# Start bytes of the activation buffers within 64 bytes, in a two-block transformer kernel on one core

## What is computed

```python
for l in range(2):                                   # first block
    z = rms_norm(x, g) @ w_in[l]                     # 1024 -> 8200 columns
    y_rg, y_ml, y_xa = rg_lru(...), mlstm(...), memory_attention(...)
    x = x + (g0*(y_rg @ w_br_rg) + g1*(y_ml @ w_br_ml) + g2*(y_xa @ w_br_xa)) @ w_out
    x = x + (swiglu(h2, w1, w3, w2) if l == 0 else moe_swiglu(h2, router, 8 experts, top 2))
for l in range(2):                                   # second block, x and a context of 256 tokens
    x = x + mod * attention(...)                     # layer 0: also for the context
    x = x + mod * swiglu_2(h_x, ffn_w1, ffn_w3, ffn_w2)
return rmsnorm(x, final_g)
```

## Time and profile before

| | us |
|---|---|
| median of 3 runs (3346.85, 3349.06, 3357.35) | 3349.06 |
| profiled execution, whole | 3353.13 |
| its span | 3351.3 |
| TensorE busy (matmuls) | 3197.1 |
| VectorE busy | 2331.1 |
| ScalarE busy | 1828.2 |
| mean granted clock of TensorE | 0.977 |

### The profile page before, as it was taken

One profiled execution on the slowest core, in us unless ns is written; L12 is line 12 of the kernel. 1 busy time (PEld: TensorE's weight loads), 2 busy tenths in 40 slices (PEclk: granted clock), 3 DMA queues, 4 the chain that ended last, 5 costly groups with the idle time before them and its releaser, 6 DMA issues.

```text
span 3351.3 us, 56010 instructions
## 1 busy us (share of the span) xinstructions
PE 3197.1 (95%) x24147; PEld 2976.5 (89%) x24147; DVE 2331.1 (70%) x2984; ACT 1828.2 (55%) x2180; POOL 0.2 (0%) x4
## 2 busy tenths in 40 slices
PE   8999999999999899999999999989899999998898
PEld 7998999999889799999999999878777889985798
DVE  6877655577876588888888888755575556466555
ACT  5564544455545477777777777643464445335443
POOL 0000000000000000000000000000000000000000
PEclk9999999999999899999999999999899999998899
DMA  6433565454335699899899999632223466530353
GB/s 256 167 131 134 178 237 201 152 194 172 115 133 181 239 380 357 334 359 357 336 356 358 338 354 356 249 132 75 102 95 129 157 236 239 214 144 33 151 187 116
DMA packets 102812, 723.62 MB, mean 216 GB/s; under 512 B 11424, under 2 KB 13344, under 8 KB 16672
## 3 DMA queue, kind: packets, MB, share of 16 engines
q1 hardware_dynamic: 102560, 719.97, 58.0%
HBM read 718.87 MB, written 1.05 MB: 215 GB/s over the span
## 4 chain that ended last, share of the span: by engine, by line
PE 78%; DVE 11%; ACT 7%; issue 2%; DMA 1%; SPq 0%; DVEq 0%; ACTq 0%
PE PS L1639 14%; PE PS L1640 14%; PE PS L1641 14%; PE PS L1590 6%; PE PS L1592 6%; PE PS L1591 6%; DVE WL L2424 4%; ACT WH L2015 3%; PE PS L1951 3%; PE PS L1952 3%; PE PS L1953 3%; PE PS L1793 1%; PE PS L1694 1%; PE PS L1721 1%; PE PS L1937 1%
## 5 line engine op out<-in xcount | busy, mean ns | idle before, releaser
L2424 DVE TENSOR_TENSOR WL<-RAW,WH 128x2048 fp32r<-128x2048 f32 (+2 forms) x428 | 962.6, 2252 | 542.1 <-ACT WH L2015 538.7
L2015 ACT ACTIVATE WH<-RAW 128x2048 fp32r<-128x2048 f32 (+2 forms) x428 | 803.5, 1880 | 243.1 <-PE PS L1641 183.0
L1639 PE MATMUL PS<-PH,WH 128*128 128x256 f32 x2464 | 703.7, 286 | 22.5 <-ACT F L2097 6.1
L1640 PE MATMUL PS<-PL,WH 128*128 128x256 f32 x2464 | 694.9, 282 | 0.0
L1641 PE MATMUL PS<-PH,WL 128*128 128x256 f32 x2464 | 694.9, 282 | 0.0
L2424 DVE TENSOR_TENSOR WL<-F,WH 128x2048 fp32r<-128x2048 f32 x210 | 480.6, 2289 | 79.9 <-ACT WH L2015 79.2
L1639 PE MATMUL PS<-HPH,WH 128*128 128x256 f32 (+1 forms) x1648 | 493.9, 300 | 17.6 <-ACT WH L2015 8.7
L1639 PEld LDWEIGHTS PS<-PH,WH 128*128 128x128 f32 x2464 | 467.1, 190 | 29.2 <-issue 20.5
L1640 PE MATMUL PS<-HPL,WH 128*128 128x256 f32 (+1 forms) x1648 | 481.6, 292 | 0.0
L1641 PE MATMUL PS<-HPH,WL 128*128 128x256 f32 (+1 forms) x1648 | 481.3, 292 | 0.0
L1640 PEld LDWEIGHTS PS<-PL,WH 128*128 128x128 f32 x2464 | 467.3, 190 | 0.6
(11 more groups left out here) (397 smaller groups left out, 4925.3 us busy)
## 6 DMA issues: line engine op xcount, KB each, us to landing
F<-in_moe_w SPq DMA_DIRECT2D x210, 1024.0 KB, 5.3
RAW<-in_ffn_w SPq DMA_DIRECT2D x130, 1024.0 KB, 5.0
RAW<-in_moe_w SPq DMA_DIRECT2D x126, 1024.0 KB, 5.1
RAW<-in_w_in SPq DMA_DIRECT2D x64, 1024.0 KB, 4.9
F<-in_ada_w SPq DMA_DIRECT2D x18, 1024.0 KB, 11.3
RAW<-in_w_kv SPq DMA_DIRECT2D x16, 1024.0 KB, 4.9
G<-in_ada_w SPq DMA_DIRECT2D x15, 1024.0 KB, 9.1
RAW<-in_w_in_ab SPq DMA_DIRECT2D x12, 1024.0 KB, 5.7
```

The lines of the kernel that those rows point to most:

```text
L1639: T_.matmul(out, lh, rh, start=first, stop=False)
L1640: T_.matmul(out, lh, rl, start=False, stop=False)
L2015: S.activation(mem["WH"][:, t.s % NHL, 0:m], v.raws[t.slot][:, 0:m], ACT.Copy).then_inc(*ac.done("w_hi", t.s))
L2424: V.tensor_tensor(mem["WL"][:, t.s % NHL, 0:m], v.raws[t.slot][:, 0:m], mem["WH"][:, t.s % NHL, 0:m].bitcast(F32), sub).then_inc(*dv.done( ...
```

## The change

P[0] to P[2] become slices of one buffer PAIRS, cut so that both halves of a pair begin 12, 20 and 26 floats further than a multiple of 4096 floats; HP and HD become one buffer each with both halves cut 6 and 2 floats past its start. By the memory map PAIRS starts where PH0 did (180064, 32 past a multiple of 64), so P[0] begins 16, P[1] 48 and P[2] 8 bytes past a multiple of 64. HP starts at 117088 as before and its halves begin 24 bytes later, 56 past. HD starts at 165536 and its halves 8 bytes later, 40 past. HP is 64 bytes longer, so what stands behind it (BIAS to G3) moves by 64 bytes; EDGE keeps G4 and G5 clear of the longer HD and moves them by 128. RAW, WH, WL and YS stay. No instruction is added, taken away or reordered; only addresses differ.

```diff
-            mem["P"] = [(sb(f"PH{i}", [128, 8, T], F32R, s1), sb(f"PL{i}", [128, 8, T], F32R, s1)) for i in range(3)]
+            pairs = sb("PAIRS", [128, 6 * 8 * T + 26], F32R, s1)
+            at = [4096 * i + first for i, first in enumerate((12, 20, 26))]
+            mem["P"] = [tuple(pairs[:, a + 2048 * j:a + 2048 * j + 2048].rearrange("p (k t) -> p k t", k=8) for j in range(2)) for a in at]
...
-        mem["HP"] = (sb("HPH", [128, 8, 512], F32R), sb("HPL", [128, 8, 512], F32R))
+        hp = sb("HP", [128, 2 * 8 * 512 + 16], F32R)
+        mem["HP"] = tuple(hp[:, 6 + 4096 * j:6 + 4096 * j + 4096].rearrange("p (k t) -> p k t", k=8) for j in range(2))
...
-            mem["G"] = [sb(f"G{i}", [128, 4, 512], F32, s3)[:, :, :] for i in range(6)]
+            mem["G"] = [sb(f"G{i}", [128, 4, 512], F32, s3)[:, :, :] for i in range(4)]
+            sb("EDGE", [128, 16], F32, s3)
+            mem["G"] += [sb(f"G{i}", [128, 4, 512], F32, s3)[:, :, :] for i in (4, 5)]
...
-            mem["HD"] = (sb("HDH", [128, 8, 512], F32R, s4), sb("HDL", [128, 8, 512], F32R, s4))
+            hd = sb("HD", [128, 2 * 8 * 512 + 16], F32R, s4)
+            mem["HD"] = tuple(hd[:, 2 + 4096 * j:2 + 4096 * j + 4096].rearrange("p (k t) -> p k t", k=8) for j in range(2))
```

## The result

The changed kernel takes **3363.67 us** (median of five runs, 3361.18 to 3365.83) beside 3349.06 us of the kernel before (five runs, 3346.85 to 3357.35). The ratio is 1.0039, with a 95% interval of 1.0027 to 1.005: slower, by 14.6 us in the medians. The forecast was 3338 us and faster; the time lies in its range and on the side of the rival "slower" (3371 us, chance 0.30). The profiled execution took 3361.18 us, its span is 3359.4 us, 8.1 more than that of before.

The account below looks back on a forecast made before the run. TensorE was taken to bound the kernel, its time near a sum of matmul start-to-start distances. Matmuls moving shifted pairs gave 10.9 us less and all other terms 0, so 3349 - 11 = 3338 us, range 3275 to 3380.

Parts of the forecast that it names:

- the rival "slower": Stream and load share interleaved banks; new distances settle the matmuls moving shifted pairs at 120 ns: 3371 us, chance 0.30.
- What bounds the kernel, and that distances from start to start are its price: TensorE, busy 3197 of 3351 us, bounds the kernel; a matmul costs its start-to-start distance, 118.33 ns for most.
- The form "rows": 118.33 to 117.5 ns, 10.9 us less: The 13104 matmuls of 256 columns that move a shifted pair gain 0.83 ns each, 10.9 us less.
- the gate tile: Matmuls with 36-column loads and stationary starts 0, 16, 32, 48 past 64; their 117.5 ns priced the new layout.
- The bounds: Router runs with 8-column loads, 114 and 120 ns: matmuls moving shifted pairs gain 57 us or lose 22.
- The form "tok": 0: The 5328 matmuls that load a shifted pair, at 116.7 to 117.7 ns, change by 0; bounds 19 less, 13 more.
- 512 columns: 0: The 1632 matmuls with 512 columns, at 233.3 ns, change by 0; bounds 9 us less, 11 us more.
- L1922, L1962, L1963: 0: Some 100 to 250 matmuls of YS with PL2 leave equal starts, 119.4 ns; under 1 us, taken as 0.
- Copies: nothing: ScalarE and VectorE copies writing the pairs at 8 mod 16 cost nothing, as convolution steps take 481 and 480 ns.
- Its second estimate: Streams from 8 mod 16 touch 65 lines, not 64; 5712 matmuls moving HP and HD cost 10 us more.
- The rival "no change": Levels come from operand order, not place, and the excess from streaming: 3349 us, chance 0.22, plus 0.02 for other residues.
- The rival "much faster": Present places keep streams slow; new ones reach the router's 114 ns, 85 us less: 3265 us, chance 0.12.

Follow-up runs that it names:

- the maps: Kernels of back-to-back matmuls alone, computation left out, against no kernel, with start bytes of moving and stationary operands varied; 256-column levels from 113.3 ns up.
- e1_map: The first kernel of matmuls alone, in stretches of 96 with operand start bytes set by hand; the windows shown have 113.3 to 120.8 ns per matmul.
- e4_p0_only: Changed kernel with HP, HD, P[1] and P[2] back at 32 past a multiple of 64, only P[0] at 16; 3350.72 us, ratio 0.9999 to the kernel before.
- e2_zero: Kernel before with a 32-byte pad ahead of all activation buffers, making pair and weight starts equal modulo 256; 3376.43 us, ratio 1.0071.
- e5_w32: Kernel before with 32 bytes ahead of WH and WL and 32 behind, moving the weights to equal starts modulo 256; 3378.27 us, ratio 1.0073.
- e8_pad64: Kernel before with a 64-byte pad ahead of all activation buffers; 3349.63 us, ratio 0.9997.
- e7_half: Kernel before with a 96-byte pad ahead of all activation buffers; 3336.12 us, ratio 0.9954.
- e10_acol: Kernel before with the 32-byte buffer ACOL moved from behind the weight tiles to ahead of WH; 3326.79 us, ratio 0.9934.
- e12_hp112: e10_acol with HP also shifted to distance 112 for its moving use, HD kept at 192; 3322.57 us, ratio 0.9916 to the kernel before.

## Why the prediction was wrong, and where it was right

*What bounds the kernel, and that distances from start to start are its price.* Right. A change of TensorE's distances by 0.4% of the time moved the time by 0.4%, DMA stayed at 0.93 in the experts (0.94 before), SyncE's wait for VectorE at 797.2 us (the earlier trace rows had 797.7), and the counts are the same.

*The form "rows": 118.33 to 117.5 ns, 10.9 us less.* **This step failed.** It measured 6.9 us more (the first five rows of the table): P[0] gained more than forecast, P[1] nothing, and P[2], HP and HD, over half of the matmuls, lost 1.7 to 2.9 ns each. The price was taken from the gate tile, which "is a mix of distances as the new kernel has one". It isn't. Its stationary operand steps by 144 bytes, so its distances are all multiples of 16, and none of the odd multiples of 8 at which P[2], HP and HD were put. With the moving operand shifted, those are the dear ones in the maps (117.5 to 122.0 ns, never 113). And its loads are of 36 columns: in e1_map a distance of 200 costs 117.8 ns with loads of 32 columns and 120.0 with 128. A mean over a mix is no price for each member of another mix. The bounds were read wrongly as well. The router's two runs have the same start bytes modulo 64 but not modulo 256: d is 224 and 192 in the run at 114 ns, 160 and 128 in the one at 120. So they don't show two patterns at equal start bytes. The measured time lies in the range only because the range was drawn wide enough for much of the rival "slower".

*The form "tok": 0.* The second failed term, and about as large: 6.6 us more. The text held that these matmuls are "around the mix" already. They stood at d 32, one of the better places (116.93 ns), and the shift of a pair changes d in both its forms, in opposite directions. To move P[0] to 16 for "rows" is to move it to 240 for "tok", and in e4_p0_only the second loses some 5 us where the first gains 4.

*512 columns: 0.* Right for this change, 233.1 and 233.3 ns, though not in general: d = 0 has 228.7. There 512 columns take 15 ns more than their columns and 256 take 13, so the excess "about doubles with the columns" only at the old distances, and the conclusion drawn from it, that most of it belongs to the streaming itself, doesn't hold as a rule.

*L1922, L1962, L1963: 0.* Right. YS and the shifted buffer are at 120.2 ns over 120 distances, 119.6 before over 121.

*Copies: nothing.* Right. ScalarE's total is 1827.9 us (1828.2), and the convolution steps that answer to the earlier trace rows take 480 and 481 ns:

```profile
L2534 DVE SCALAR_TENSOR_TENSOR TMP<-PS,PAR,TMP 128x255 f32<-128x255 f32 x16 | 7.7, 481 | 6.6 <-ACT TMP L2105 6.5
...
L2534 DVE SCALAR_TENSOR_TENSOR TMP<-PS,PAR,TMP 128x253 f32<-128x253 f32 x16 | 7.7, 480 | 0.6
```

*The rival "slower"* named the sign and two facts that hold: equal starts are bad (120.0 ns, e2_zero and e5_w32), and its point of decision, 118.8 ns for the form "rows". The mean of the 12800 starts came to 118.9. Its size, 22 us from the form "rows", came near the 14.6 us by luck: that form lost 6.9, and the other half came from the form "tok". Its reason, that 32 is halfway from the worst distance and every other is nearer to it, isn't borne out: the period is 256, and with it 112 and 192 are better than 32 and 72 is worse than 0 (form "rows"). Its second estimate, 10 us for the extra 16-byte line of a stream from 8 mod 16 ("SBUF — State Buffer", "Door 1: The DMA port swizzle", of the Trainium skill), is close to the 9.5 us that HP and HD measure. The maps agree with it in size: a moving operand 8 past a multiple of 16 costs 1.8 ns more in the mean than a stationary one at the same d, and the estimate was 1.85. Still the rule alone doesn't carry it: the difference goes from -0.6 ns (d 40) to 4.2 (d 248), and d = 0, where no stream begins inside a line, costs the same 120.0.

*The rival "no change"* fell by e8_pad64, e2_zero and e5_w32. The Trainium skill has two independent SBUF read ports for TensorE ("TensorE: Matmul & The Clock Gate", "Step-by-step: what each phase is for"). The trace disagrees in this much: with nothing altered but start bytes, and all of them multiples of 32, the stream's spacing goes from 113.3 ns (d 64, e7_half) to 120.0 (d 0, e2_zero), so load and stream are not without effect on each other.

*The rival "much faster"* was right that the fast pattern can be had at full loads: 113.3 ns. The change didn't reach it but for about a quarter of P[0]'s "rows". The price of 57 us for it was too high, since the best means over a kind of "rows" starts were 114.0 (HD, e10_acol) and 114.1 (HP, e12_hp112). No window here came below 113.3 ns. The Trainium skill gives the formula behind 109.2 ns ("TensorE: Matmul & The Clock Gate", "Back-to-back issue gap") for an isolated matmul and says that in a stream with loads the spacing is set by both, so it was no forecast for these streams.

## What to carry to other kernels

Where TensorE is busy for 95% of the span, the start byte of a buffer is a knob of a few per cent of a stream: take for each kind of product the distance from moving operand to the next stationary operand, modulo 256. Try 192 with both at multiples of 32, or 112 with the moving operand 16 past a multiple of 32 and the stationary one at a multiple of 32 (the other way round it costs 119.8 ns). Avoid 0, and avoid a moving operand that begins 8 past a multiple of 16. Moving one buffer of 32 bytes gave 0.7% here, and five odd offsets lost 0.4%. Cost both forms in which a buffer is used, since its shift has the opposite sign in the other. And don't price a new layout by the mean over another mix: a small kernel of matmuls alone gave the levels of the full kernel to within a quarter of a nanosecond at most distances, as long as the same operand was the shifted one.

## What was not expected of the hardware

**The spacing depends on the two start bytes with a period of 256 bytes.** The DMA share doesn't move it: P[0] "tok" at d 240 has 118.4 ns beside a DMA share of 0.88, the map 118.2 to 118.4 beside next to none. At multiples of 32 the difference d sets the levels. At the others it also matters which operand is off its multiple of 32. Mean ns for 256 columns:

| d | in a kernel | alone, moving operand shifted | alone, stationary operand shifted |
|---|---|---|---|
| 0 | 119.9 | 119.8 | 119.8 |
| 8 | 117.7 (tok) | 117.5, 117.8, 120.0 | 117.6 |
| 16 | 113.4, 116.7, 118.7 (rows) | 113.5, 118.7 | 117.3, 119.7 |
| 32 | 116.9 | 116.8 | 116.8 |
| 40 | 120.0 (rows) | 119.3 | 119.5 to 120.0 |
| 48 | 118.3 (rows) | 118.3 | 116.7 (once 120.0) |
| 64 | 113.3, 117.8 | 113.3, 117.8 | 113.3, 117.8 |
| 72 | 121.2 (rows) | 121.1 to 121.9 | 117.8, 120.0 |
| 112 | 113.4 (mean 114.1, rows) | 113.5 to 114.9 | 119.7 to 120.0 |
| 144 | 119.8 (tok) | 116.7, 118.7 | 119.8 to 120.2 |
| 184 | 118.5 (tok) | 120.0 | 118.3 |
| 192 | 113.3, 117.8 | 113.4, 117.8 | 113.7, 117.8 |
| 224 | 118.3 | 118.3 | 118.3 |
| 240 | 118.3 (tok) | 117.1 | 118.3 |
| 248 | 120.0 (rows) | 120.0 | 115.7 to 116.3 |

"rows" in a kernel is the moving operand shifted, "tok" the stationary one, and each agrees with the column of its own side within 0.3 ns, but for 116.7 at d 16 and 120.0 at d 40.

**At some distances a stream has two or three stable patterns,** and at d 16, 64 and 192 the one it enters it keeps, for as much as 1466 distances (HP and then HD in e10_acol). At d 112 a stream settles instead: in e12_hp112 the first 24 distances have 115 to 116 ns in many stretches, all after them 113.3. That would be why 112 came out low at every entry. At 2.4 GHz 113.33, 116.67, 118.33 and 120.00 ns are 272, 280, 284 and 288 columns' times, the columns themselves being 256. What picks one lies in how the stream is entered, and it repeats: in the changed kernel P[0]'s stretches at 355.30 and at 1026.32 us, the same code of the first and of the second layer, both have 113.52 ns, those at 344.02 and 1015.04 both 116.69. Which property of the entry it is stays open, and with it whether a kernel can steer it. Why the period is 256, why the place within 32 bytes counts, and why 512 columns prefer 0, 64 and 112 (229 to 230 ns in the kernels, 233 at 32, 192 and 224), wasn't settled either; no run looked inside a memory access.
